# Weight sums for a seven-product multiply, formed by adding DMAs in device memory and loaded as slabs of their own, on six slabs of eleven

## The reference, cut to what matters

```python
def swiglu_2(h, w_in, w_out):
    gate, up = jnp.split(h @ w_in, 2, axis=-1)
    return (jax.nn.silu(gate) * up) @ w_out
...
    for l in range(DEPTH):
        x = x + 0.5 * swiglu_2(rms_norm(x, ffn1_norm[l]), ffn1_w_in[l], ffn1_w_out[l])
        h = rms_norm(x, mix_norm[l]) @ w_mix_in[l]
        ...
        x = x + 0.5 * swiglu_2(rms_norm(x, ffn2_norm[l]), ffn2_w_in[l], ffn2_w_out[l])
```

## Time and profile before

| | |
|---|---|
| median of 3 runs | 1642.88 us (1642.75 to 1643.07) |
| profiled execution | 1642.93 us; its span 1641.6 us |
| busy share of the span | TensorE 99%, VectorE 75%, ScalarE 52%, GpSimd 18% |
| DMA | 346 MB, 211 GB/s in the mean; GpSimd's queue 17 MB of it |
| slabs of w_out | 88 DMAs of 512 KB (four stages of eleven slabs), median 4.1 us to landing |

### The profile page before, as it was taken

How to read it: one execution, slowest core, us unless ns; L and a number is a source line. 1 busy time by engine, 2 the same in 40 slices (tenths; PEclk the granted TensorE clock), 3 DMA queues, 4 the chain that set the end, 5 groups by cost and what they waited for, 6 DMA issues and landing times.

```text
span 1641.6 us, 21147 instructions
## 1 busy us (share of the span) xinstructions
PE 1619.2 (99%) x7872; PEld 1309.4 (80%) x7872; DVE 1226.6 (75%) x1476; ACT 850.7 (52%) x1062; POOL 292.8 (18%) x429
## 2 busy tenths in 40 slices
PE   6999999999999999999999999999999999999999
PEld 3776788888778888788888878888888888888887
DVE  3898778897787674766978776688667978866686
ACT  3436654435475443645656554454545647564453
POOL 0001000000002240134403002450044204003350
PEclk9999999999999999999999999999999999999999
DMA  9784398898638876577665428766676664347661
GB/s 350 242 289 169 106 318 278 309 353 264 205 123 268 272 251 196 175 232 225 200 189 180 129 80 248 224 198 220 200 215 211 216 199 158 103 129 233 215 212 52
DMA packets 250295, 346.22 MB, mean 211 GB/s; under 512 B 16160, under 2 KB 197124, under 8 KB 250192
## 3 DMA queue, kind: packets, MB, share of 16 engines
q1 hardware_dynamic: 236288, 323.00, 59.8%
q0 software_dynamic: 11472, 17.34, 4.5%
q10 hardware_dynamic: 2432, 4.51, 0.8%
HBM read 329.32 MB, written 1.05 MB: 201 GB/s over the span
## 4 chain that ended last, share of the span: by engine, by line
PE 89%; DVE 5%; ACT 3%; issue 1%; DMA 1%; SPq 0%; DVEq 0%; ACTq 0%
PE bank L491 21%; PE bank L493 21%; PE bank L492 21%; PE bank L898 5%; PE bank L903 5%; PE bank L899 5%; DMA raw<-in_ada_w 1%; DVE lo L2059 1%; PE bank L1411 1%; PE bank L1412 1%; PE bank L1414 1%; PE bank L846 1%; PE bank L1219 1%; ACT hi L1467 1%; DVE XN L2545 1%
## 5 line engine op out<-in xcount | busy, mean ns | idle before, releaser
L2059 DVE TENSOR_TENSOR lo<-raw,hi 128x2048 fp32r<-128x2048 f32 x230 | 528.2, 2300 | 194.2 <-ACT hi L1467 193.9
L1467 ACT ACTIVATE hi<-raw 128x2048 fp32r<-128x2048 f32 x242 | 462.0, 1914 | 248.0 <-PE bank L493 173.0
L491 PE MATMUL bank<-hi,XTh 128*128 128x512 f32 (+1 forms) x1424 | 558.8, 392 | 1.7 <-DVE XTl L2216 1.3
L493 PE MATMUL bank<-hi,XTl 128*128 128x512 f32 (+1 forms) x1424 | 551.4, 387 | 0.0
L492 PE MATMUL bank<-lo,XTh 128*128 128x512 f32 (+1 forms) x1424 | 550.9, 387 | 0.0
L491 PEld LDWEIGHTS bank<-hi,XTh 128*128 128x128 f32 x1424 | 267.4, 188 | 65.9 <-issue 12.5
L493 PEld LDWEIGHTS bank<-hi,XTl 128*128 128x128 f32 x1424 | 267.4, 188 | 55.2
L492 PEld LDWEIGHTS bank<-lo,XTh 128*128 128x128 f32 x1424 | 267.6, 188 | 53.8 <-issue 1.0
L3153 POOL DMA_DIRECT2D HTR<-BLK x320 | 192.4, 609 | 624.7 <-DVE BLK L2647 585.2
L898 PE MATMUL bank<-hi,HTh 128*128 128x512 f32 x400 | 156.6, 391 | 0.0
L899 PE MATMUL bank<-lo,HTh 128*128 128x512 f32 x400 | 155.7, 389 | 0.0
(11 more groups left out here) (420 smaller groups left out, 1862.8 us busy)
## 6 DMA issues: line engine op xcount, KB each, us to landing
raw<-in_ffn_w_in SPq DMA_DIRECT2D x176, 512.0 KB, 4.9
raw<-in_ffn_w SPq DMA_DIRECT2D x132, 512.0 KB, 5.0
raw<-in_ada_w SPq DMA_DIRECT2D x96, 512.0 KB, 5.5
raw<-in_ffn_w_out SPq DMA_DIRECT2D x88, 512.0 KB, 4.1
raw<-in_w_mix_in SPq DMA_DIRECT2D x52, 512.0 KB, 4.7
raw<-in_od_pw_w SPq DMA_DIRECT2D x24, 512.0 KB, 6.2
HTR<-BLK POOLq DMA_DIRECT2D x240, 48.0 KB, 3.9
raw<-in_ev_w_in SPq DMA_DIRECT2D x20, 512.0 KB, 9.8
```

Source lines behind the costliest of these rows:

```text
L491: pe.matmul(dst, xh, wh, start=start, stop=False)
L493: return pe.matmul(dst, xl, wh, start=False, stop=stop)
L1467: act.activation(hi[r][:, :], raw[g % RAW][:, :], ACT.Copy).then_inc(*up("hi", d))
L2059: dve.tensor_tensor(lo[r][:, :], raw[g % RAW][:, :], hi[r][:, :].bitcast(F32), ALU.subtract).then_inc(*up("lo", d))
```

## The change

Six slabs of eleven (`FASTS = (0, 1, 3, 4, 6, 7)`) go by seven products in each of the four stages. The sums of weight quarters are no longer formed on VectorE. For each stage there is an array in device memory (`sums3`, `sums5`, `sums6`, `sums8`; one 128 x 2048 slab for each fast slab). GpSimd copies the two weight tiles of a slab there, and then adds with DMAs (`accum_op`) until it holds four sums: w00 + w01, w01 + w11, the sum of all four quarters, and w00 + w01 + w11. Six DMAs make one slab; two slabs go together in four steps, each of which waits for the DMAs of the step before. The signs of the scheme are turned so that only additions are needed (`column_sums` and `shared_sums` change signs to fit). The finished slab is loaded and split like any weight slab, right behind its fast slab, of which three quarters are still loaded. So a down part has 17 ring places in place of 11 (`down_at`, `down_order`). `SH` is now three tiles, `SL` lies over `SR` in another order, and the chunks at which columns are split are listed anew. VectorE's shared sums and ScalarE's copy for them stand behind the splits of the last fast slab.

```diff
+    def fast_slab(w, s):
+        def parts(slot):
+            d = slot[:, :].rearrange("p (k n) -> p k n", k=2)
+            return [(d[:, 0, 0:512], w[2 * s * P:(2 * s + 1) * P, 0:512]), (d[:, 1, :], w[(2 * s + 1) * P:(2 * s + 2) * P, :])]
+        add(parts)
+
+    def sums_slab(p, i):
+        def parts(slot):
+            return [(slot[:, n * D:(n + 1) * D], A["sums"][p][i, :, n * D:(n + 1) * D]) for n in range(2)]
+        add(parts)
...
-FASTS = (1, 3, 5, 7)
-FAST_SPLIT_UP = {5: (0,), 6: (1, 2), 8: (4,), 9: (3, 5), 10: (6,)}
-FAST_BATCH = {n: [i for i, s in enumerate(FASTS) if s in batch] for n, batch in enumerate(BATCHES)}
+FASTS = (0, 1, 3, 4, 6, 7)
+FAST_SPLIT_UP = {5: (2,), 6: (0, 1), 8: (5,), 9: (3, 4)}
+FAST_SPLIT_DOWN = {1: (8,), 2: (6, 7), 4: (9, 10)}
+FAST_BATCH = {n: [i for i, s in enumerate(FASTS) if s in batch] for n, batch in enumerate(BATCHES[:3])}
...
             def seven(f, d, s, i):
...
-                pe.wait_ge(*at("t_hi", (f, i)))
-                pe.wait_ge(*at("t_lo", (f, i)))
-                three(bank[3][:, :], *x_sum(0), *w_sum(0), begin, end)
-                three(bank[1][:, :], *x_sum(2), *w_sum(1), begin, end)
-                three(bank[0][:, :], *x_sum(1), *w_sum(2), begin, end)
-                return three(acc[1][0][:, :], *x(1, 1), *w_sum(3), False, False)
+                three(acc[0][1][:, :], *x_sum(3), *w(1, 1), begin, False).then_inc(*up("used", d))
+                ready(d + 1)
+                three(bank[3][:, :], *x_sum(0), *w_sum(0), begin, end)
+                three(acc[1][0][:, :], *x(1, 1), *w_sum(2), begin, False)
+                if begin:
+                    pe.wait_ge(*at("hidden", (f, NC - 1, 1)))
+                three(bank[1][:, :], *x_sum(2), *w_sum(1), begin, end)
+                three(bank[0][:, :], *x_sum(1), *w_sum(3), begin, end).then_inc(*up("used", d + 1))
...
             def down(p, late, after=None):
                 nslab, d = DOWNS[p][0], first[f"down{p}"]
-                f = FFNS[p - 1] if p - 1 in FAST else None
-                if f is not None:
-                    weights_low(f, 0)
-                    weights_sums(f, d, 1)
-                for s in range(nslab - 3):
-                    if late is not None and s == 0:
+                for j, s, n in down_order(p)[:-3]:
+                    if late is not None and j == d:
                         late()
-                    if f is not None and s in FASTS[:-1]:
-                        weights_low(f, FASTS.index(s) + 1)
-                    if f is not None and s == FASTS[-1]:
-                        shared_sums(f)
-                    split(d + s + RING)
-                    if f is not None and s + RING in FASTS[2:]:
-                        weights_sums(f, d, FASTS.index(s + RING))
-                    if after:
+                    split(j + RING)
+                    if after and n == 0:
                         after(s)
+                if p - 1 in FAST:
+                    shared_sums(FFNS[p - 1])
                 rows(p, 0)
...
         def gpsimd_engine(pool):
+            def weights_sums(p):
+
+                l, kind = (p - 3) // 3, "ffn1" if p in (3, 6) else "ffn2"
+                w = A[f"{kind}_w_out_2"][l, :, :].rearrange("(s k p) n -> s k p n", k=2, p=P)
+                for n, own in FAST_BATCH.items():
+                    for i in own:
+                        v = A["sums"][p][i, :, :]
+                        pool.dma_start(v[:, 0:D], w[FASTS[i], 0, :, :]).then_inc(*up("sums_part", (p, i, 0), 16))
+                        pool.dma_start(v[:, D:SLAB], w[FASTS[i], 1, :, :]).then_inc(*up("sums_part", (p, i, 1), 16))
+                    pool.wait_ge(*at("sums_part", (p, own[-1], 1)))
+                    for i in own:
+                        v = A["sums"][p][i, :, :]
+                        pool.dma_start(v[:, 0:512], w[FASTS[i], 0, :, 512:D], accum_op=ALU.add).then_inc(
+                            *up("sums_part", (p, i, 2), 16))
+                        pool.dma_start(v[:, 512:D], w[FASTS[i], 1, :, 512:D], accum_op=ALU.add).then_inc(
+                            *up("sums_part", (p, i, 3), 16))
+                    pool.wait_ge(*at("sums_part", (p, own[-1], 3)))
+                    for i in own:
+                        v = A["sums"][p][i, :, :]
+                        pool.dma_start(v[:, D + 512:SLAB], v[:, 0:512], accum_op=ALU.add).then_inc(
+                            *up("sums_part", (p, i, 4), 16))
+                    pool.wait_ge(*at("sums_part", (p, own[-1], 4)))
+                    for i in own:
+                        v = A["sums"][p][i, :, :]
+                        pool.dma_start(v[:, D:D + 512], v[:, D + 512:SLAB], accum_op=ALU.add).then_inc(
+                            *up("sums_made", (p, i), 16))
+                    pool.wait_ge(*at("sums_made", (p, own[-1])))
...
             for g in range(4):
                 o = (g % 2) * HD
                 pool.dma_start(WB[o:o + HD, g // 2, o:o + HD], A["ev_fourier_w"][0, g, :, :]).then_inc(*up("four_w", g, 16))
+            weights_sums(3)
             pool.wait_ge(*at("o_full", 3))
...
             pool.dma_start(ZA[PERIOD:PERIOD + 1, :, :, :], A["conv_bias"]).then_inc(*up("conv_in", 3, 16))
+            weights_sums(5)
             move_blocks(2)
...
+                weights_sums((6, 8)[l])
                 move_blocks(3 * l + 5)
...
+                if split in sums_at:
+                    sp.wait_ge(*at("sums_made", (sums_at[split], FAST_BATCH[fast_batch(fast_at[split - 1][1])][-1])))
```

More of the change, by code:

```diff
@@ L120, in weight_slabs @@
 def weight_slabs(A):
-    slabs, first, dense = [], {}, []
+    slabs, first, dense, fast_at, sums_at = [], {}, [], {}, {}
     up0 = 2 * len(COLS5) + len(DOWN0)
@@ L453, in col @@
             return COLS[:, vec[name]:vec[name] + n]
-        slabs, first, dense = weight_slabs(A)
+        A["sums"] = {p: nc.dram_tensor(f"sums{p}", (len(FASTS), P, SLAB), F32, kind="Internal").ap() for p in FAST}
+        slabs, first, dense, fast_at, sums_at = weight_slabs(A)
         quarter_at = {g: key[1:] for key, g in first.items() if key[0] == "ada"}
-        fast_at = {first[f"down{p + 1}"] + s: (FFNS[p], i) for p in FAST for i, s in enumerate(FASTS)}
         def fox_stat(i, o, n):
@@ L467, in mix_columns, with down_at, down_order, fast_batch @@
             return UM[:, t, a:a + 2 * (b - a)].rearrange("p (x n) -> p x n", x=2)[:, :, 0:HALF]
+        def down_at(p, s):
+            return first[f"down{p}"] + s + (sum(x < s for x in FASTS) if p - 1 in FAST else 0)
+        def down_order(p):
+            kinds = [(s, (0, 1) if p - 1 in FAST and s in FASTS else (0,)) for s in range(DOWNS[p][0])]
+            return [(down_at(p, s) + n, s, n) for s, parts in kinds for n in parts]
+        def fast_batch(i):
+            return next(n for n in FAST_BATCH if i in FAST_BATCH[n])
+        def sums_slot(i):
+            return (i + 4) % 8
+        def sums_own(n):
+            i = FAST_BATCH[n][0]
+            return slice(sums_slot(i), sums_slot(i) + len(FAST_BATCH[n]))
         def sums_of(p):
@@ L906, in down @@
                 for s in range(1 if p == 0 else 0, nslab - 3):
-                    ready(d + s)
                     if before:
                         before(s)
-                    if d + s in fast_at:
-                        seven(*fast_at[d + s][:1], d, s, fast_at[d + s][1]).then_inc(*up("used", d + s))
-                    elif head is not None and s == 0:
+                    if down_at(p, s) in fast_at:
+                        seven(FFNS[p - 1], down_at(p, s), s, FASTS.index(s))
+                        continue
+                    ready(down_at(p, s))
+                    if head is not None and s == 0:
                         products(s, 1)
@@ L917, in down @@
                         products(s, 0)
-                        products(s, 1).then_inc(*up("used", d + s))
+                        products(s, 1).then_inc(*up("used", down_at(p, s)))
                     if late is not None and s == 0:
@@ L935, in down @@
                             if m == 1:
-                                last.then_inc(*up("used", d + s))
+                                last.then_inc(*up("used", down_at(p, s)))
                         if m == 0:
@@ L939, in down @@
                     return
-                products(nslab - 3, 1).then_inc(*up("used", d + nslab - 3))
+                products(nslab - 3, 1).then_inc(*up("used", down_at(p, nslab - 3)))
                 if p < 9 and not normed_first(p):
@@ L2530, in residual @@
                 else:
-                    dve.wait_ge(*at("used", first[f"down{p}"] + DOWNS[p][0] - 1))
+                    dve.wait_ge(*at("used", down_at(p, DOWNS[p][0] - 1)))
                 if p - 1 in FAST:
@@ L2616, in down @@
                 else:
[L2617 removed]
+                    split(down_at(p, nslab - 3) + RING)
                     rows(p, 1)
@@ L3206, in sync_engine @@
```

(2 more changed lines are left out.)

151 lines of the change are left out of this document (61 added, 90 removed).

## The result

The changed kernel takes 1660.22 us (median of 4 runs, 1656.17 to 1661.32) against 1642.97 us before: a ratio of 1.0101, 95% interval 1.0083 to 1.0119. It is 17 us slower; the forecast was 1638.0, that is 5 us faster. The profiled execution took 1659.27 us, its span 1658.0. Of the rivals the slower one came true.

What follows compares the result with a forecast made beforehand. TensorE, busy 1619.2 of 1641.6 us, was taken as the bound. From 1642.93 us, 5.44 us of matmuls came off (1637.5), 0.5 us was added for thin places, GpSimd's sums cost nothing: 1638.0 us, own range 1636.9 to 1639.6, high end 1662.

Steps and rivals of the forecast that it cites:

- slower rival: Adding DMAs slower than taken, GpSimd's order delaying block moves: from about 65 us a set; 1673 us at 75; chance 0.32.
- The gain: TensorE in four down stages: eight slabs go from 24 to 21 matmuls, 5.44 us off, all on the path.
- VectorE and ScalarE in the down parts: Splits and shared sums stay off TensorE's path, with thin margins of 0.8 us (third slab) and 0.3 us (stage end).
- The 0.5 us charge: Added for the two thin places, a stage's third slab and the shared sums at its end, together.
- the rival of a gain given back: Inside the four stages, VectorE 1 us later in each makes TensorE wait 4 us: 1641.5 us, no change; chance 0.18.
- The size of a set: One stage's 36 GpSimd DMAs in three batches: 98 us alone, 62 us DMA time; copy 1.5 loads, addition 2.
- 16 moves take 9.8 us and land 3.9 us later: GpSimd's block moves of ffn 2, behind ffn 5's sums: landing at 532.4, 25 us of slack; similar slack for ffn 5, 8.
- loads may lag ... about 18 us: Feed-forward stage after ffn 3's sums: weight loads may lag about 18 us, the four-place ring included, at no cost.
- 29 is below 13 + 18 = 31: ffn 3's sums spill 29 us of DMA time; 13 us spare plus 18 us lag cover it, costing nothing, narrowly.
- The set of ffn 5: GpSimd's sums from 396.5 us, ahead of ffn 2's moves: mean 129 us against 147 allowed, costing nothing.
- late by more than 25 us: Sign of a wrong forecast: moves of ffn 2, 5 or 8 starting that late after the DMA sums.
- Matmuls waiting for hi or lo: Sign of a wrong forecast: TensorE waiting for split weight slabs between 205 and 380 us.

Runs made afterwards that it cites:

- the kernel without sets: Changed kernel with no sums formed by GpSimd; the sums slabs are loaded from w_out itself: 1637.82 us, ratio 0.9967.
- the spread kernels: Changed kernel with its twelve DMA batches moved elsewhere in GpSimd's list: 1649.78 us; also ffn 6's third batch later 1637.49, shared sums earlier 1645.35, both 1637.42.
- set 5 alone: Changed kernel forming only ffn 5's sums, slabs of ffn 3, 6 and 8 loaded from w_out: 1639.37 us median, 1637.76 to 1645.86.
- the late start alone: Against the kernel without sets: GpSimd's block moves of ffn 5 and 8 wait for TensorE's first slab of chunk 5: 1645.38 us.

## Why the prediction was wrong, point by point

- **The gain**: right. 1.36 and 1.37 us in ffn 3 and ffn 6, where the starts above show it apart, and 5.4 for all four stages in the kernel without sets.
- **VectorE and ScalarE in the down parts**: right. The 0.5 us charge was not needed; the rival of a gain given back fell.
- **The size of a set**: right in the sum, by luck: two errors cancel. DMA time 62 us foreseen, 60 to 62 measured; a copy costs 1.0 to 1.06 loads and not 1.5, an addition 2.3 to 2.5 and not 2, all within the bounds. The Trainium skill (DMA: Bandwidth & Descriptors, Latency and other measured facts) gives 214 GB/s as the full rate of copies; by that, an estimate, a set of copies alone would need 59 us, and the run shows 37.5 us. The lengths came out as 134 us (129 by 3 x 43), 141 (129), 128 (124) and 128 us (124).
- **"16 moves take 9.8 us and land 3.9 us later"**: this is the step that failed for ffn 5 and 8. I took the first group of ffn 2, which has no pause. The first group of ffn 5, which it was to stand for, has one: the last row is a single move of ffn 5, and the next rows of that view, of the kernel before, have the other 15 after 2.50 us of "issue", and the first instruction that reads them:

```profile
1014.17 9.11 POOL L3153 DMA_DIRECT2D HTR<-BLK  x15 [2.50 <-issue]
1027.45 2.20 POOL L3132 TENSOR_TENSOR SR<-HTR 128x128 f32<-128x128 f32 x1 [4.18 <-DMA HTR<-BLK]
```

  Already there the moves are done 16.4 us after the first is issued, not 13.7, which leaves the set 126 us and not 129. Behind a set, in the change, the 16 take 17.8 us in ffn 5 and 20.0 in ffn 8, and the last lands 1.4 us after. That is 5.5 and 7.6 us more than the 13.7 reckoned, so the slack was 18.5 and 16.4 us, and the sets had 123.5 and 121.4 us. At 128 us TensorE stops 3.65 us in ffn 5, and 5.3 in ffn 8. The sets ended inside what I allowed; the allowance was wrong.
- **"loads may lag ... about 18 us", "29 is below 13 + 18 = 31"**: this is the step that failed for ffn 0. The spill itself was less than foreseen: the third batch and the last steps of the second, some 20 + 4 us of DMA time. TensorE lost 7.8 us all the same. The allowance counted the ring of four as cover, as if only TensorE waited for a late slab. But ScalarE and VectorE keep their order, and the activation and the product of a finished chunk stand behind the late split (248.78 and 251.07 above); so the ring's 12 us were no cover. Without them the allowance is 13 + 6 = 19 us, and 24 is over it. This is read from the timeline; no run changed the order on ScalarE and VectorE in ffn 0. What a run does show is that the third batch is the cause: in the spread kernels, with that batch moved out of ffn 0 and only the two last steps of the second past 200 us, ffn 0 lost nothing.
- **The set of ffn 5**: 25 us of slack foreseen, the same mis-sized moves (16.5 us here), and a length that varies: 141 us in the change, 148 in the profiled execution of set 5 alone, where 147 were allowed. It costs from nothing to 8 us from run to run.
- **No term for the clock.** The stops sum to 15.5 us with the 0.7 of ffn 2, the loss is 22; the difference is, within half a microsecond, the 6.9 us of busy time above: matmuls at the lower level behind the longer stops. TensorE in the chain of waits, right behind the stop in ffn 5 (start, us):

```profile
1063.22 0.80 PE bank L529
1064.02 0.43 PE bank L530
1064.44 0.43 PE bank L531
...
1066.45 0.23 PE bank L530
```

  Matmuls 0.43 us apart, then 0.23 again: the two levels, 1.2 and 2.4 GHz.
- **The signs named in advance.** Moves "late by more than 25 us" was the wrong mark: they came 23.5 us late (1041.83 against 1011.05 + 7.3) and that was too much. "Matmuls waiting for hi or lo" did not come either; they waited for HID.
- The Trainium skill (DMA: Bandwidth & Descriptors, Issuing engines are not separate DMA queues) was cited for the slower rival, and the trace agrees: slabs of the first block's feed-forward stages (raw<-in_ffn_w) land in 8.0 us in the median, 5.0 before.

The slower rival named the mechanism and both places, but priced its onset at 65 us of DMA time a set; it set in at 60 to 62, because the room was smaller than reckoned on both counts. The measured 1660.2 us lies below the 1662 of the forecast's high end, but only because that end was put there for this rival; the sum itself went the wrong way.

## What to carry to other kernels

When work is put ahead of something that has slack, measure the slack on the slowest instance of the chain in the trace, pauses of the issuing engine included, and compare it with the upper end of the new work, not its mean. A late load is not covered by a deep ring where the same in-order engine also finishes or frees what earlier work is waiting for: ask what stands behind the late instruction in each list. Work with a distant deadline belongs in several gaps: the same bytes and the same instructions in other places took 1637.5 us instead of 1660.2.

## What the runs showed of the hardware

A stop of TensorE costs more than its length: behind stops of 2.1 to 8.7 us the granted clock of a 20 us stretch was 0.77 to 0.91, while in the stretch with the 0.7 us wait in ffn 2 it stayed at 1.00. An adding DMA within device memory took 2.3 to 2.5 times, a plain copy 1.0 to 1.06 times the DMA time of a load of the same bytes. GpSimd's moves pause for 2 to 7 us, shown as "issue", in 6 to 13 of the 20 groups of every kernel, and the pauses of a stage stand 20 moves apart: in the kernel before after moves 20 and 40 in ffn 2, 3 and 6, and after moves 1, 21 and 41 in ffn 5 and 8. Behind the sets of ffn 6 and 8 a second row of them joins, after moves 8 and 28; with the steps of the third batch issued between the groups the four groups of ffn 5 ran without one (9.3 to 10.0 us). With the late start alone they stood where they stand without sets. So the places go with what GpSimd issued before, not with the time; what causes these pauses was not tried, and it stays open.
